# A gated recurrence over 256 tokens: doubling levels in place of sixteen sub-chunks and a chain of states

## Chip, cores and metric

One core of one Trainium2 chip runs the whole kernel. The metric is the device time of one execution in microseconds; the median of three runs is used. All data are fp32.

## The reference, cut to what matters

The model is two transformer blocks over 256 tokens of width 1024. The first has differential attention, a pooling mixer, 32 experts and an embedding gate. The second has windowed attention, a gated recurrence and 32 smaller experts. The change concerns the recurrence of the second block, four heads with 128 keys and 128 values:

```python
fg = lb + (1.0 - lb) * jax.nn.sigmoid(f_h)        # forget gates
hq = jax.nn.silu(q_h)
hk = 1.0 - fg
hlogf = jnp.log(fg)
hv = i_h
...
def step(state, inp):                             # chunks of 64 tokens
    b = jnp.cumsum(gc, axis=2)
    o_inter = jnp.einsum('bhtk,bhkv->bhtv', qc * jnp.exp(b), state)
    decay = jnp.exp(jnp.where(causal, b[t] - b[s], -jnp.inf))
    a = jnp.einsum('bhtk,bhsk,bhtsk->bhts', qc, kc, decay)
    o_intra = jnp.einsum('bhts,bhsv->bhtv', a, vc)
    state = jnp.exp(b_last) * state + (kc * jnp.exp(b_last - b))^T vc
...
ho = rms_norm_2(hgrn2_chunkwise(hq, hk, hv, hlogf), hgrn_norm_w)
hgrn = ho * jax.nn.silu(g_h)
mixed = sigmoid(z_a) * (attn @ w_branch_attn) + sigmoid(z_b) * (hgrn @ w_branch_hgrn)
x = x + mixed @ w_out
```

Written out, the output of token t is the sum over s up to t of (q_t · (product of the gates after s up to t) · k_s) v_s, the product being taken per key channel.

## The kernel before

The kernel is written by hand, engine by engine, with semaphores. Weights stream through a ring of six slots of 2 MB, filled by SyncE in a fixed order; each load waits until the last matmul that reads the slot's old content has run. The six slots serve first the projections of block one, then the experts of block one, then the seventeen loads of the middle, then the experts of block two. In block two an expert takes three slots, and each slot's next load waits for a count of TensorE's (`free[s]`). The first six expert loads wait for `dense2`, a count of finished dense products.

The middle of block two runs on TensorE as follows. Norm and transposes; twenty projections (`project(i)`, two row tiles for each piece of `w_in`), each eight matmuls of 128x512, into banks 0 to 3 in turn. ScalarE copies each out or takes its sigmoid (`leave(i)`). Between them stand the score matmuls of the attention, the transposes of its probabilities (L1583, copied by VectorE at L1056) and its products with the values (L1591).

The recurrence of before splits the 256 tokens into sixteen sub-chunks of 16 (`SUB`). Inside a sub-chunk it works by offset: for n = 0 to 15 VectorE forms the products of query and key of all token pairs whose key stands at one position (`offset(n)`, L1095 and L1099) and TensorE sums them over the keys' channels by a matmul with a shifted matrix of ones (`sums(n)`, L1615). Across sub-chunks a state of 128x128 for each head goes from one to the next: TensorE makes the update (`update(i)`, L1626), VectorE applies the gates (`state(i)`, L1114), and TensorE multiplies the state by the queries (`inter(i)`, L1635). The eight-plus-eight matmuls of the last piece of `w_in` (`last_projections`, L1649) are put one by one between these. Then the products of the pair matrix with the values (L1673) are added, the output is copied and transposed back (L1681), normalized on VectorE, and multiplied by the gate.

After it come the branch products from L1492, which is the line of the helper `dense` for every dense product of the middle, the transposes, the output projection, the router and the experts (gate and up at L1346, down at L1373).

Of the kernel before, what the change touches and what calls it, by code (L numbers as in the profile page):

```python
# [45 lines left out]
SUB = 16  # L46
NSUB = T // SUB
# [7 lines left out]
def two_blocks(nc, w, out):  # L55
# [11 lines left out]
    with ctx:  # L67
# [15 lines left out]
        blk = sb("blk", [P, P])  # L83
        spread = sb("spread", [P, P + SUB - 1])
# [3 lines left out]
        par = sb("par", [P, 2])  # L88
# [171 lines left out]
        k1, pre_f, suf_f, r_q, w_a, w_b, q_e, ke_even, ke_odd = (scr[:, 1024 * k:1024 * (k + 1)] for k in range(9))  # L260
        by_sub = "p (b j) -> p b j"
        states = xs[:, :, :].rearrange("p a n -> p (a n)").rearrange("p (k n) -> p k n", k=4)
# [60 lines left out]
        def _(pool):  # L323
# [20 lines left out]
            pool.memset(tri[:, :], 1.0)  # L344
            step(pool.memset(blk[:, :], 1.0))
# [4 lines left out]
            select(blk[:, :], ALU.is_ge, 0.0, 0, [[-SUB, P // SUB], [0, SUB]], 1)  # L350
            select(blk[:, :], ALU.is_ge, 0.0, SUB - 1, [[SUB, P // SUB], [0, SUB]], -1)
# [26 lines left out]
            step(pool.memset(spread[:, :], 0.0))  # L378
            pool.memset(spread[:, SUB - 1::SUB], 1.0)
# [12 lines left out]

            step(pool.tensor_copy(par[:, 1:2], blk[:, SUB:SUB + 1]))
            for k in (3, 5, 7):
                step(pool.tensor_tensor(par[:, 1:2], par[:, 1:2], blk[:, SUB * k:SUB * k + 1], ALU.add))
            pool.tensor_tensor(par[:, 0:1], ones[:, 0:1], par[:, 1:2], ALU.subtract).then_inc(sem("parity"), 1)
# [7 lines left out]
        def _(act):  # L404
# [205 lines left out]
            for a in range(TT):  # L610
                act.activation(xs[:, 1, 512 * a:512 * (a + 1)], Z[:, a, 1280:1792], ACT.Sigmoid).then_inc(sem("g_sig"), 1)

            act.wait_ge(sem("row_max"), 3)
            for g in range(8):
                act.activation(sA0[:, g, :], sA0[:, g, :], ACT.Exp, bias=qss[:, g:g + 1],
                               accum_out=qms[:, g:g + 1]).then_inc(sem("probs"), 1)
            for i in range(12, 16):
                leave(i)
            act.wait_ge(sem("row_max"), 4)
            for g in range(8):  # L620
                act.activation(sA1[:, g, :], sA1[:, g, :], ACT.Exp, bias=qss[:, 8 + g:9 + g],
                               accum_out=qms[:, 8 + g:9 + g]).then_inc(sem("probs"), 1)
            act.activation(qrt[:, 0:16], qrt[:, 0:16], ACT.Exp).then_inc(sem("sink_exp"), 1)
            for i in range(16, 20):
                leave(i)

            act.wait_ge(sem("hgrn_o"), 1)
            act.copy(w_b[:, 0:512], bank(0)).then_inc(sem("oT_act"), 1)
# [11 lines left out]
        def _(dve):  # L640
# [387 lines left out]
            step(tt(hq, hq, xs[:, 0, :], ALU.mult))  # L1028

# [13 lines left out]
            for a, sc in enumerate((sA0, sA1)):  # L1043
                m = qrs[:, 8 * a:8 * a + 8]
                step(dve.tensor_reduce(m, sc, X, ALU.max))
                step(tt(m, m, sinks[:, :], ALU.max))
                step(tt(qrt[:, 8 * a:8 * a + 8], sinks[:, :], m, ALU.subtract))
                ts(qss[:, 8 * a:8 * a + 8], m, -1.0, None, ALU.mult).then_inc(sem("row_max"), 1)
            dve.wait_ge(sem("g_sig"), 2)
            for a in range(TT):  # L1050
                v = Z[:, a, 1280:1792]
                step(tt(v, v, xs[:, 1, 512 * a:512 * (a + 1)], ALU.mult))

            for k in range(6):
                dve.wait_ge(sem("w_turned"), 3 + k + 1)
                dve.tensor_copy(pT2[:, 4 * k:4 * k + 4, :], bank(4 + k % 4).rearrange("p (g q) -> p g q", g=4))\  # L1056
                    .then_inc(sem("p2_copied"), 1)

            step(ts(k1, fg, -1.0, 1.0, ALU.mult, ALU.add))
            f_b, k_b, r_b = (v.rearrange(by_sub, j=SUB) for v in (fg, k1, r_q))  # L1060
            pf_b, sf_b = (v.rearrange(by_sub, j=SUB) for v in (pre_f, suf_f))
            wa_b, wb_b = (v.rearrange(by_sub, j=SUB) for v in (w_a, w_b))
            factor, start = xs[:, 0, :], xs[:, 1, :]
            factor_b, start_b = (v.rearrange(by_sub, j=SUB) for v in (factor, start))
            dve.tensor_copy(factor, fg)
            step(dve.memset(start, 0.0))
            dve.memset(factor_b[:, :, 0:1], 0.0)
            step(dve.tensor_copy(start_b[:, :, 0:1], f_b[:, :, 0:1]))
            step(dve.tensor_tensor_scan(pre_f, factor, start, 0.0, ALU.mult, ALU.add))
            step(dve.memset(sf_b[:, :, SUB - 1:SUB], 1.0))  # L1070
            for j in range(SUB - 1, 0, -1):
                step(tt(sf_b[:, :, j - 1:j], sf_b[:, :, j:j + 1], f_b[:, :, j:j + 1], ALU.mult))
            tt(suf_f, suf_f, k1, ALU.mult).then_inc(sem("ke_ready"), 1)
# [4 lines left out]
            for a in range(TT):  # L1078
                dve.wait_ge(sem("pv"), 2 + a + 1)
                tt(ao[:, a, :].rearrange("p (g d) -> p g d", d=64), bank(6 + a).rearrange("p (g d) -> p g d", d=64),  # L1080
                   qrs[:, 8 * a:8 * a + 8, None].broadcast_to([P, 8, 64]), ALU.mult).then_inc(sem("branch_ready"), 1)
            for a in range(TT):
# [3 lines left out]
            step(tt(q_e, hq, pre_f, ALU.mult))  # L1086

            step(dve.tensor_copy(r_q, hq))
            nb = TT * P * 4 // SUB

            def offset(n):
                j = SUB - 1 - n
                if n:
                    v = r_b[:, :, j + 1:SUB]
                    step(tt(v, v, f_b[:, :, j + 1:j + 2].broadcast_to([P, nb, SUB - 1 - j]), ALU.mult))  # L1095
                if n >= 2:
                    dve.wait_ge(sem("w_used"), n - 1)
                buf = (wa_b, wb_b)[n % 2]
                tt(buf[:, :, j:SUB], r_b[:, :, j:SUB], k_b[:, :, j:j + 1].broadcast_to([P, nb, SUB - j]), ALU.mult)\  # L1099
                    .then_inc(sem("w_offset"), 1)  # L1100

            def state(i):

                dve.wait_ge(sem("update"), i + 1)
                if i >= 4:
                    dve.wait_ge(sem("inter"), i - 3)
                new, old = states[:, (i + 1) % 4, :], states[:, i % 4, :]
                if i == 0:
                    dve.tensor_copy(new, bank(5)).then_inc(sem("state"), 4)
                    return  # L1110
                dve.wait_ge(sem("state"), 4 * i)
                for n in range(4):
                    r = slice(n * P, (n + 1) * P)
                    stt(out=new[:, r], in0=old[:, r], scalar=pre_f[:, n * T + SUB * i + SUB - 1:n * T + SUB * i + SUB],  # L1114
                        in1=bank(5 + 2 * (i % 2))[:, r], op0=ALU.mult, op1=ALU.add).then_inc(sem("state"), 1)

            offset(0)
            offset(1)
            dve.wait_ge(sem("parity"), 1)
            for a in range(TT):  # L1120
                dve.wait_ge(sem("ke_turned"), a + 1)
                for v, k in ((ke_even, 0), (ke_odd, 1)):
                    ts(v[:, 512 * a:512 * (a + 1)], bank(7 if a == 0 else 5), par[:, k:k + 1], None, ALU.mult)\
                        .then_inc(sem("ke_copied"), 1)
            for n in range(2, SUB):
                offset(n)
                state(n - 2)

            dve.wait_ge(sem("w_used"), SUB)
            for g in range(2):  # L1130
                tt(r_q[:, 512 * g:512 * (g + 1)].rearrange("p (g t) -> p g t", g=4), bank(4 + 2 * g).rearrange("p (g t) -> p g t", g=4),
                   blk[:, None, :].broadcast_to([P, 4, P]), ALU.mult).then_inc(sem("intra"), 1)
            state(NSUB - 2)
            dve.wait_ge(sem("hgrn_o"), 2)
            dve.tensor_copy(w_b[:, 512:1024], bank(1)).then_inc(sem("oT_dve"), 1)

            for a in range(TT):
                dve.wait_ge(sem("o_turned"), a + 1)
                step(dve.tensor_copy(k1[:, 512 * a:512 * (a + 1)], bank(6 + a)))
            o = k1.rearrange("p (g d) -> p g d", d=P)  # L1140
# [598 lines left out]
```

## Time and profile before

| | |
|---|---|
| median of 3 runs | 1975.18 us (1974.69 to 1977.14) |
| profiled execution | 1973.43 us |
| its span | 1971.7 us |
| TensorE matmul busy | 1776.4 us (90%) |
| VectorE busy | 429.3 us (22%) |
| ScalarE busy | 261.3 us (13%) |
| DMA, mean over the span | 339 GB/s |
| mean granted TensorE clock | 0.976 |

The profile cuts the span into 40 slices of 49.3 us; slices are counted from 0 here. Busy shares are averages over stages of very different kinds, so the chain of waits and the timelines of single stretches count for more. fp32 matmuls and their weight loads appear as two records each; transposes as one. The busy time of a matmul record overlaps its neighbours', so starts are compared, not durations added.

### The profile page before, as it was taken

To read this page: it belongs to the slowest core of one execution; us is meant where nothing else is said; L and a number is where in the kernel's file an instruction comes from. 1 tells how busy PE (TensorE), PEld (TensorE's weight loads), DVE (VectorE), ACT (ScalarE), POOL (GpSimd) and SP (SyncE) were. 2 spreads that over 40 slices of the span, in tenths; PEclk is the share of its full clock that TensorE was granted. 3 is DMA by queue.
4 is the path that set the end of the run, shared out by engine and by line. 5 is a ranking of instruction groups with operands and counts; after the bars stand their busy time and mean duration, and the time that the engine had idled before them with its cause. 6 is when DMAs were issued, how large, how long until landed. Compare 5 with 4: busy or idle time off the path is not lost.

```text
span 1971.7 us, 28706 instructions
## 1 busy us (share of the span) xinstructions
PE 1776.4 (90%) x12236; PEld 822.3 (42%) x12236; DVE 429.3 (22%) x1033; ACT 261.3 (13%) x534; POOL 24.4 (1%) x100
## 2 busy tenths in 40 slices
PE   7778999999999999999999988989988888888887
PEld 3444333333333333333333335647645555555554
DVE  1623111111111111111111123226523111111111
ACT  1210111111111111111111021130011111111111
POOL 3010000000000000000000000000000000000000
PEclk9888999999999999999999998999998999999999
DMA  9424999999999999999999783330144999999997
GB/s 302 177 75 176 429 428 429 428 428 429 427 430 427 429 428 428 429 428 428 428 429 429 308 298 128 128 128 1 69 150 157 428 429 427 429 428 429 428 428 309
DMA packets 69697, 667.73 MB, mean 339 GB/s; under 512 B 9392, under 2 KB 11200, under 8 KB 31648
## 3 DMA queue, kind: packets, MB, share of 16 engines
q1 hardware_dynamic: 64864, 664.84, 81.0%
q10 hardware_dynamic: 4416, 1.49, 0.3%
q0 software_dynamic: 384, 0.93, 0.2%
q8 instruction: 24, 0.39, 0.1%
q14 instruction: 9, 0.07, 0.0%
HBM read 666.19 MB, written 1.05 MB: 338 GB/s over the span
## 4 chain that ended last, share of the span: by engine, by line
DMA 50%; PE 43%; DVE 3%; ACT 1%; issue 1%; SPq 1%; DVEq 0%; ACTq 0%
DMA ring<-in_w_up 34%; DMA ring<-in_w_up_experts 16%; PE ps L1319 13%; PE ps L1492 11%; PE ps L1346 4%; PE ps L1198 3%; PE ps L1304 2%; PE ps L1373 2%; PE ps L1267 2%; PE ps L1615 1%; PE ps L1182 1%; PE ps L1626 1%; PE ps L1649 1%; PE ps L1392 1%; PE ps L1635 1%
## 5 line engine op out<-in xcount | busy, mean ns | idle before, releaser
L1319 PE MATMUL ps<-ring,Z 128*64 128x512 f32 x3168 | 710.3, 599 | 36.5 <-DMA ring<-in_w_up 35.8
L1319 PEld LDWEIGHTS ps<-ring,Z 128*64 128x64 f32 x3168 | 218.9, 137 | 501.6 <-issue 416.0
L1346 PE MATMUL ps<-ring,Z 128*32 128x128 f32 x4096 | 246.9, 408 | 64.4 <-DMA ring<-in_w_gate_experts 33.0
L1346 PEld LDWEIGHTS ps<-ring,Z 128*32 128x32 f32 x4096 | 148.4, 126 | 153.9 <-DMA ring<-in_w_up_experts 44.4
L1492 PE MATMUL ps<-ring,xT 128*128 128x512 f32 (+1 forms) x352 | 147.7, 580 | 1.5 <-DVE xT L662 0.8
L875 DVE TENSOR_SCALAR Z<-ps 128x512 f32<-128x512 f32 x33 | 22.8, 692 | 437.7 <-PE ps L1319 437.7
L1304 PE MATMUL ps<-xs,Z 128*32 128x256 f32 (+1 forms) x800 | 105.6, 476 | 4.5 <-DVE Z L847 4.5
L1492 PEld LDWEIGHTS ps<-ring,xT 128*128 128x128 f32 x352 | 67.5, 193 | 79.1 <-issue 76.2
L877 DVE TENSOR_SCALAR Z<-ps 128x512 f32<-128x512 f32 x33 | 22.8, 692 | 250.8 <-PE ps L1319 250.8
L887 DVE TENSOR_TENSOR Z<-Z,ps 128x128 f32<-128x128 f32 x32 | 9.2, 288 | 296.6 <-ACT Z L502 296.6
L515 ACT COPY Z<-ps 128x512 f32<-128x512 f32 (+1 forms) x65 | 31.2, 480 | 290.6 <-PE ps L1319 247.1
L506 ACT COPY Z<-ps 128x256 f32<-128x256 f32 x65 | 24.2, 372 | 340.5 <-PE ps L1354 340.5
L1392 PE MATMUL ps<-Z 64*128 64x512 f32 x264 | 65.6, 615 | 1.5 <-ACT Z L515 1.5
L1373 PE MATMUL ps<-ring,Z 128*32 128x256 f32 x1024 | 61.6, 379 | 0.0
L1198 PE MATMUL ps<-ring,xT 128*128 128x512 f32 x128 | 57.5, 612 | 0.8 <-DVE xT L662 0.8
L860 DVE TENSOR_TENSOR Z<-ps,gcol 128x512 f32<-128x512 f32 (+1 forms) x67 | 37.5, 560 | 83.7 <-PE ps L1313 83.5
L1304 PEld LDWEIGHTS ps<-xs,Z 128*32 128x32 f32 (+1 forms) x800 | 37.1, 126 | 41.7 <-issue 27.0
L1182 PE MATMUL ps<-ident,xs 128*128 128x128 f32 x112 | 21.0, 361 | 36.8 <-DVE xs L658 29.5
L499 ACT ACTIVATE Z<-Z 128x512 f32<-128x512 f32 x33 | 20.8, 630 | 238.4 <-DVE Z L875 238.4
L502 ACT ACTIVATE Z<-ps 128x128 f32<-128x128 f32 x32 | 8.9, 277 | 301.5 <-PE ps L1346 301.5
L868 DVE TENSOR_SCALAR Z<-iota,Z 128x128 f32<-128x128 f32 x130 | 38.9, 341 | 31.4 <-PE ps L1354 31.4
L1373 PEld LDWEIGHTS ps<-ring,Z 128*32 128x32 f32 x1024 | 36.9, 109 | 19.1 <-issue 0.2
(356 smaller groups left out, 1250.8 us busy)
## 6 DMA issues: line engine op xcount, KB each, us to landing
ring<-in_w_gate SPq DMA_DIRECT2D x66, 2048.0 KB, 23.0
ring<-in_w_up SPq DMA_DIRECT2D x66, 2048.0 KB, 25.6
ring<-in_w_down SPq DMA_DIRECT2D x66, 2048.0 KB, 21.4
ring<-in_w_gate_experts SPq DMA_DIRECT2D x32, 2048.0 KB, 17.0
ring<-in_w_up_experts SPq DMA_DIRECT2D x32, 2048.0 KB, 21.5
ring<-in_w_down_experts SPq DMA_DIRECT2D x32, 2048.0 KB, 13.0
ring<-in_w_in SPq DMA_DIRECT2D x13, 2048.0 KB, 9.6
ring<-in_w_out SPq DMA_DIRECT2D x4, 2048.0 KB, 17.3
```

The source lines that it names most:

```text
L515: act.copy(y[:, 0:(512, 256)[k]], bank((7, 5)[k])[:, 0:(512, 256)[k]]).then_inc(done_by(q, "act", "y"), 1)
L860: tt(picked[:, 0:DC * CAPS[k]].rearrange("p (c j s) -> p c j s", **by_chunk), bank(6)[:, 0:DC * CAPS[k]].rearrange("p (c j s) -> p c j s", ...
L868: ts(gated[:, a].rearrange("p (j s) -> p j s", s=CAPS[k]), iota[:, None, 0:CAPS[k]].broadcast_to([P, P // CAPS[k], CAPS[k]]), rank[:, a, d ...
L1182: last = pe.transpose(dst[:, i * P:(i + 1) * P], src[:, c + i:c + i + stride * (P - 1) + 1:stride], ident[:, :])
L1198: last = pe.matmul(bank((4 + j) % 8), xT[:, c, a * P:(a + 1) * P], slot(u, DC, 512)[:, c, :], start=c == 0, stop=c == DC - 1)
L1267: last = pe.matmul(bank((5, 6, 7, 0)[b]), xT[:, c, a * P:(a + 1) * P], slot(4 + n, DC, 512)[:, c, :], start=c == 0, stop=c == DC - 1)
L1304: last = pe.matmul(bank(6)[n * j:n * (j + 1), 0:P * c].rearrange("p (q c) -> p q c", c=c), one_hot[:, a, 0:n], xs[:, a, :].rearrange("p (q ...
L1319: last = pe.matmul(dst[CAP * j:CAP * (j + 1)], lhsT, rhs(j), start=start, stop=True, skip_group_check=True)
L1346: last = pe.matmul(bank(4)[CAP2 * t:CAP2 * (t + 1), P * s:P * (s + 1)], picked[:, chunk * CAP2:(chunk + 1) * CAP2], v[:, c, t:512:4], star ...
L1373: last = pe.matmul(bank(5)[CAP2 * t:CAP2 * (t + 1), 0:T], hid[:, CAP2 * j:CAP2 * (j + 1)], v[:, j, T * t:T * (t + 1)], start=j == 0, stop= ...
L1392: last = pe.matmul(bank(2 * a + j), back[CAP * j:CAP * (j + 1), a * P:(a + 1) * P], y[CAP * j:CAP * (j + 1), :], start=False, stop=True, s ...
L1492: last = pe.matmul(dst, lhs(c), rhs(c), start=c == 0, stop=c == nc_ - 1)
```

## The change

The recurrence is computed for all 256 tokens by doubling. `q_e` starts as query times own gate and `k_e` as one minus the gate. At level k the tokens are seen in pairs of blocks of 2^k. The product of `k_e` with the second blocks' `q_e` (one matmul of 128 by 128 by 64 for each head and row tile) holds the wanted entries for the pairs of that level; a mask `pair` of that level picks them into `own_A` by a predicated copy. Then `q_e` of the second blocks is multiplied by the gates' product over the first block, and `k_e` of the first blocks by that over the second; `totals` holds these products, halved in number at each level. Seven levels cover a row tile of 128. One set of products between the tiles (`cross_products`) and the diagonal (`own_products`, picked by multiplication with the identity) complete the matrix. Twelve matmuls with the values give the output in token rows, in banks 6 and 7, so it isn't transposed back.

Around it: projections use banks 0 and 1 in turn in place of 0 to 3; levels stand between the last projections on TensorE, the transposes of the probabilities are split in two and four; all exponentials of the attention stand ahead of projection 12's copy on ScalarE; the sum of squares of the output is ScalarE's; the norm's gain is multiplied into the gate beforehand; GpSimd builds `pair` in place of the block mask, the matrix of shifted ones and the parities.

```diff
+        q_e, k_e = xs[:, 0, :], xs[:, 1, :]
...
+            step(pool.memset(pair[:, :, :], 1.0))
+            for level in range(LEVELS - 1):
+                n = 2 ** level
+                v = pair[:, level, :].rearrange("p (b j) -> p b j", j=n)
+                select(v, ALU.is_ge, 0.0, 0, [[-2 * n, P // 2 // n], [0, n]], 1)
+                select(v, ALU.is_ge, 0.0, n - 1, [[2 * n, P // 2 // n], [0, n]], -1)
...
-                b, a = bank(i % 4), i % 2
+                b, a = bank(i % 2), i % 2
...
-            for i in range(12, 16):
+            for a, sc in enumerate((sA0, sA1)):
+                act.wait_ge(sem("row_max"), 3 + a)
+                for g in range(8):
+                    act.activation(sc[:, g, :], sc[:, g, :], ACT.Exp, bias=qss[:, 8 * a + g:8 * a + g + 1],
+                                   accum_out=qms[:, 8 * a + g:8 * a + g + 1]).then_inc(sem("probs"), 1)
+            act.activation(qrt[:, 0:16], qrt[:, 0:16], ACT.Exp).then_inc(sem("sink_exp"), 1)
+            for i in range(12, 18):
                 leave(i)
...
+            ts(k_e, fg, -1.0, 1.0, ALU.mult, ALU.add).then_inc(sem("level"), 1)
+            tt(q_e, hq, fg, ALU.mult).then_inc(sem("level"), 1)
...
+            def level(k):
+                size = 2 ** k
+                dve.wait_ge(sem("products"), k + 3)
+                dve.wait_ge(sem("level"), 2 * k + 2)
+                whole = totals[k].rearrange("p (b two) -> p b two", two=2)
+                n = whole.shape[1]
+                if k < LEVELS - 1:
+                    dve.tensor_tensor(totals[k + 1], whole[:, :, 0], whole[:, :, 1], ALU.mult).then_inc(sem("total"), 1)
+                for v, other in ((q_e, 0), (k_e, 1)):
+                    v = split(v, size)[:, :, 1 - other, :]
+                    tt(v, v, whole[:, :, other, None].broadcast_to([P, n, size]), ALU.mult).then_inc(sem("level"), 1)
+                if k < LEVELS - 1:
+                    dve.copy_predicated(split(own_A, size)[:, :, 1, :].rearrange("p (g b) j -> p g b j", g=8),
+                                        pair[:, k, None, :].bitcast(I32).broadcast_to([P, 8, P // 2]).rearrange("p g (b j) -> p g b j", j=size),
+                                        bank(2 + k % 2).rearrange("p (g b j) -> p g b j", g=8, j=size)).then_inc(sem("chosen_A"), 1)
+                else:
+                    dve.tensor_copy(split(own_A, size)[0:size, :, 1, :],
+                                    bank(2 + k % 2)[0:size, :].rearrange("p (g j) -> p g j", j=size)).then_inc(sem("chosen_A"), 1)
...
+            for a in range(TT):
+                v = Z[:, a, 1280:1792]
+                step(tt(v, v, g_sig[a], ALU.mult))
+                v = v.rearrange("p (g d) -> p g d", d=P)
+                tt(v, v, hnorm[:, None, :].broadcast_to([P, 4, P]), ALU.mult).then_inc(sem("g_silu"), 1)
+            for k in range(3):
+                level(k)
+            copy_p(range(2))
+            for k in range(3, 5):
+                level(k)
+            copy_p(range(2, 6))
+            level(5)
...
+            def products(k):
+                size = 2 ** k
+                pe.wait_ge(sem("level"), 2 * k + 2)
+                pe.wait_ge(sem("chosen_A"), k + 1)
+                rows = P if k < LEVELS - 1 else size
+                for n in range(4):
+                    for a in range(TT):
+                        g = n * TT + a
+                        last = pe.matmul(bank(2 + k % 2)[0:rows, g * 64:(g + 1) * 64].rearrange("p (b j) -> p b j", j=size),
+                                         tokens(k_e, n, a)[:, 0:rows], split(tokens(q_e, n, a), size)[:, :, 1, :],
+                                         start=True, stop=True)
+                last.then_inc(sem("products"), 1)
...
+            own_products()
+            project(11)
+            products(0)
+            project(12)
+            products(1)
+            project(13)
+            products(2)
+            turn_p(range(2))
+            project(14)
+            products(3)
+            project(15)
+            products(4)
+            turn_p(range(2, 6))
+            project(16)
+            products(5)
```

After these stand the products of probabilities and values, project(17), products(6), the transposes of the attention output, project(18), cross_products, project(19) and the products with the values; `offset`, `state`, `sums`, `update`, `inter` and `last_projections` are gone.

## Rows read from the trace of the kernel before

**Rows 1.** The page: DMA share by slices, and the chain by engine.
```profile
DMA  9424999999999999999999783330144999999997
...
DMA 50%; PE 43%; DVE 3%; ACT 1%; issue 1%; SPq 1%; DVEq 0%; ACTq 0%
```

**Rows 2.** The chain that ended last, in order: start us, us, what.
```profile
1268.94 41.41 PE ps L1492 x96
...
1333.87 5.32 PE ps L1591 x48
...
1351.89 0.61 PE ps L1615 x4
...
1353.39 0.80 PE ps L1635 x8
...
1406.43 1.88 PE ps L1673 x16
...
1411.05 13.75 PE ps L1492 x32
...
1549.36 21.79 DMA ring<-in_w_up_experts
```

**Rows 3.** SyncE's queue: first, last preload of experts, and the seventh load.
```profile
1405.66 0.33 SPq L283 DMA_DIRECT2D ring<-in_w_gate_experts  x1
...
1472.31 0.43 SPq L283 DMA_DIRECT2D ring<-in_w_down_experts  x1
1506.24 0.34 SPq L288 DMA_DIRECT2D ring<-in_w_gate_experts  x1
```

**Rows 4.** Busy us by stretch: length, PE, PEld, DVE, ACT, POOL, clock, DMA.
```profile
1343.60:1411.00 67.40, 66.47 (x365) 49.99 (x366) 41.62 (x95) 3.06 (x4) 0.00 (x0) 0.97 0.07 24
1411.00:1502.00 91.00, 75.33 (x245) 38.26 (x243) 37.43 (x104) 8.02 (x17) 1.80 (x2) 0.92 0.33 123
```

**Rows 5.** Groups by line, TensorE, 1343 to 1411 us.
```profile
L1615 PE MATMUL ps<-scr,spread 128*128 128x32 f32 (+15 forms) x64 | 20.0, 436 | 1.0 <-DVE scr L1099 1.0
...
L1626 PE MATMUL ps<-Z,scr 32*128 32x128 f32 x120 | 17.0, 282 | 0.0
```

**Rows 6.** TensorE's timeline: start, us, group, and the idle before it.
```profile
1310.17 1.04 PE L1583 MATMUL ps<-ident,scr 128*128 128x128 f32 x8
1316.38 3.68 PE L1583 MATMUL ps<-ident,scr 128*128 128x128 f32 x16 [5.17 <-ACT scr L621]
...
1341.58 1.06 PE L1604 MATMUL ps<-ident,scr 128*128 128x128 f32 x8 [0.88 <-DVE Z L1084]
1343.65 0.79 PE L1615 MATMUL ps<-scr,spread 128*128 128x32 f32 x4 [1.01 <-DVE scr L1099]
```

**Rows 7.** Line L1591: duration ns, minimum, median, maximum.
```profile
L1591 PEld LDWEIGHTS ps<-Z,scr x48: 190/192/192, 1333.3 to 1338.8; 128*128 128x128 f32 x48
```

**Rows 8.** VectorE's timeline.
```profile
1266.46 1.29 DVE L1032 SCALAR_TENSOR_TENSOR scr<-ps,mask_win 128x512 f32<-128x512 f32 x2 [10.80 <-PE ps L1557]
...
1284.70 1.42 DVE L1052 TENSOR_TENSOR Z<-Z,xs 128x512 f32<-128x512 f32 x2 [9.79 <-ACT xs L611]
...
1317.53 0.69 DVE L1056 COPY scr<-ps 128x512 f32<-128x512 f32 x1 [5.36 <-PE ps L1583]
```

**Rows 9.** ScalarE's timeline.
```profile
1283.52 1.15 ACT L611 ACTIVATE xs<-Z 128x512 f32<-128x512 f32 x2
1284.69 1.28 ACT L615 ACT_TABLE_LOAD   x1
...
1312.79 0.49 ACT L621 ACTIVATE scr<-scr,st 128x256 f32<-128x256 f32 x1
```

**Rows 10.** As rows 4, short stretches: the granted clock is third from the end.
```profile
1318.00:1320.00 2.00, 2.00 (x11) 2.00 (x10) 1.60 (x3) 0.00 (x0) 0.00 (x0) 0.50 0.48 181
...
1345.00:1347.00 2.00, 2.00 (x7) 1.24 (x6) 1.97 (x5) 0.00 (x0) 0.00 (x0) 0.50 0.00 0
...
1380.00:1390.00 10.00, 10.00 (x55) 7.49 (x55) 6.72 (x15) 0.00 (x0) 0.00 (x0) 1.00 0.00 0
```

More of the change, by code:

```diff
@@ L259, in two_blocks, with split @@
         hq, fg = Z[:, 0, 3840:4864], Z[:, 1, 3840:4864]
-        k1, pre_f, suf_f, r_q, w_a, w_b, q_e, ke_even, ke_odd = (scr[:, 1024 * k:1024 * (k + 1)] for k in range(9))
-        by_sub = "p (b j) -> p b j"
-        states = xs[:, :, :].rearrange("p a n -> p (a n)").rearrange("p (k n) -> p k n", k=4)
+        q_e, k_e = xs[:, 0, :], xs[:, 1, :]
+        own_A = scr[:, 0:1024]
+        cross_A = scr[:, 7424:7936].rearrange("p (n t) -> p n t", n=4)
+        o2 = scr[:, 2304:3328]
+        o2_sq = scr[:, 3328:4352]
+        g_sig = [Z[:, a, 3328:3840] for a in range(TT)]
+        def split(v, size):
+            return v.rearrange("p (b two j) -> p b two j", two=2, j=size)
+        totals, at = [fg], 0
+        for level in range(LEVELS - 1):
+            n = T * 4 >> (level + 1)
+            totals.append(hq[:, at:at + n])
+            at += n
         full = [sem(f"slot_full{s}") for s in range(SLOTS)]
@@ L1102, in state @@
[L1102 to L1115, printed above, removed]
@@ L1130, in _ @@
[L1130 to L1139, printed above, removed]
@@ L1585, in _, with tokens, own_products @@
-            for i in range(16, 18):
-                project(i)
+            project(10)
+            def tokens(v, n, a):
+                return v[:, n * T + a * P:n * T + (a + 1) * P]
+            def own_products():
+                pe.wait_ge(sem("level"), 1)
+                for a in range(TT):
+                    for n in range(4):
+                        last = pe.matmul(bank(2 + a)[:, n * P:(n + 1) * P], tokens(k_e, n, a), tokens(hq, n, a), start=True, stop=True)
+                    last.then_inc(sem("products"), 1)
@@ new lines, in cross_products, with turn_p @@
+            def cross_products():
+                pe.wait_ge(sem("level"), 2 * LEVELS + 2)
+                pe.wait_ge(sem("chosen_A"), LEVELS + 1)
+                for n in range(4):
+                    last = pe.matmul(bank(3)[:, n * P:(n + 1) * P], tokens(k_e, n, 0), tokens(q_e, n, 1), start=True, stop=True)
+                last.then_inc(sem("products"), 1)
+            def turn_p(ks):
+                for k in ks:
+                    g0 = 4 * (k % 2)
+                    if k == 0:
+                        pe.wait_ge(sem("scores2_copied"), 6)
+                    if k in (0, 2):
+                        pe.wait_ge(sem("probs"), 24 if k == 0 else 32)
+                    if k >= 4:
+                        pe.wait_ge(sem("p2_copied"), k - 3)
+                    for i in range(4):
+                        src = sA0[:, g0 + i, :] if k < 2 else sA1[:, g0 + i, (k // 2 - 1) * P:(k // 2) * P]
+                        last = pe.transpose(bank(4 + k % 4)[:, i * P:(i + 1) * P], src, ident[:, :])
+                    last.then_inc(sem("w_turned"), 1)
@@ L1608, in sums @@
-            def sums(n):
-                j = SUB - 1 - n
-                pe.wait_ge(sem("w_offset"), n + 1)
-                buf = (w_a, w_b)[n % 2].rearrange(by_sub, j=SUB)
-                nb = 512 // SUB
-                for g in range(2):
-                    last = pe.matmul(bank(4 + 2 * g).rearrange(by_sub, j=SUB)[:, :, j:SUB], spread[:, n:n + P],
-                                     buf[:, nb * g:nb * (g + 1), j:SUB], start=n == 0, stop=True, skip_group_check=True)
-                last.then_inc(sem("w_used"), 1)
@@ L1619, in update @@
-            def update(i):
-                if i >= 2:
-                    pe.wait_ge(sem("state"), 4 * (i - 1))
-                a, r = i // 8, slice(32 * (i // 2 % 4), 32 * (i // 2 % 4) + 32)
-                src = (ke_even, ke_odd)[i % 2]
-                for n in range(4):
-                    last = pe.matmul(bank(5 + 2 * (i % 2))[:, n * P:(n + 1) * P], src[r, 512 * a + n * P:512 * a + (n + 1) * P],
-                                     Z[r, a, 768 + n * P:768 + (n + 1) * P], start=True, stop=True)
-                last.then_inc(sem("update"), 1)
@@ L1630, in inter @@
-            def inter(i):
-                pe.wait_ge(sem("state"), 4 * i)
-                for n in range(4):
-                    lo = (n % 2) * T + SUB * i
-                    last = pe.matmul(bank(n // 2)[:, lo:lo + SUB], states[:, i % 4, n * P:(n + 1) * P],
-                                     q_e[:, n * T + SUB * i:n * T + SUB * (i + 1)], start=False, stop=True,
-                                     skip_group_check=True)
-                    if i == NSUB - 1 and n % 2 == 1:
-                        last.then_inc(sem("hgrn_o"), 1)
-                if i < NSUB - 1:
-                    last.then_inc(sem("inter"), 1)
@@ L1643, in last_projections @@
-            def last_projections(n):
-                a, c = n // DC, n % DC
-                if c == 0:
-                    pe.wait_ge(*middle_full(12))
-                    pe.wait_ge(sem("d2_copied"), 15 + a)
-                last = pe.matmul(bank(2 + a), tile(a)(c), slot(12 % SLOTS, DC, 512)[:, c, :], start=c == 0, stop=c == DC - 1)
-                if c == DC - 1:
-                    last.then_inc(sem("dense2"), 1)
-            sums(0)
-            last_projections(0)
-            sums(1)
@@ L1656, in _ @@
-            last_projections(1)
-            pe.wait_ge(sem("ke_copied"), 4)
-            pe.wait_ge(sem("d2_copied"), 18)
-            for b in range(2):
-                pe.matmul(bank(b), zeros[:, :], q_e[:, 0:512], start=True, stop=True)
-            update(0)
-            update(1)
-            for n in range(2, SUB):
-                sums(n)
-                last_projections(n)
-                inter(n - 1)
-                if n < NSUB - 1:
-                    update(n)
-            pe.wait_ge(sem("intra"), 2)
@@ L1684, in _ @@
+                    last = pe.matmul(out_o, by_tile[:, n, a, :], Z[:, a, v_n], start=True, stop=a == 0)
+                    if a == 1:
+                        last = pe.matmul(out_o, cross_A[:, n, :], Z[:, 0, v_n], start=False, stop=True)
+                last.then_inc(sem("hgrn_o"), 1)
             pe.wait_ge(*middle_full(13))
             pe.wait_ge(sem("d2_copied"), 20)
+            pe.wait_ge(sem("branch_copied"), 2)
             v_a, v_h = slot(13 % SLOTS, 4, 1024), slot(14 % SLOTS, 4, 1024)
```

168 lines of the change are left out of this document (53 added, 115 removed).

## Prediction

> **What bounds the kernel now.** I read the page first. Half of the chain that ended last is DMA and most of the rest is TensorE [rows 1]. The slices of the DMA line say where: the two stages of experts run with the DMA engines full, and between them, in slices 24 to 30, the engines are mostly idle. The change lies in that middle. So the first question is whether time won there reaches the end, for some 430 us of transfers stand behind it.
>
> The chain in order of time answers it [rows 2]. From 1268.9 us to 1411.1 us it is TensorE almost alone. Later, inside the second expert stage, it becomes transfers of in_w_up_experts, 21.8 us a piece. The queue of SyncE shows what starts these transfers [rows 3]. The first six fill the ring while the middle still runs (issued at 1405.7 to 1472.3 us). The seventh is issued at 1506.2 us, when TensorE has freed slot 0 with the first expert's gate matmuls. All later ones hang on it. Nothing in the stream starts at a time of its own: each wait counts something TensorE has done. If the branch products start earlier by x, the six preloads, the first expert and the seventh transfer all come earlier by x, and so does the end. Between the sixth preload and the seventh transfer lie 34 us, and the DMA engines are busy for a third of the time around them [rows 4], so the ring is full when the first expert starts, and stays so when all of it moves together.
>
> Then the stretch itself. Between the end of the score matmuls (1268.9) and the first branch product (1411.1) lie 142.1 us. TensorE is busy for 66.5 of the last 67.4 us, VectorE for 41.6 [rows 4]: the recurrence is not bound by VectorE, it is made of TensorE's small matmuls. In it stand, one by one, the 16 matmuls of the last two projections (L1649). They remain.
>
> **The change, part by part.** I compute TensorE's work between the same two points afterwards, then check that no other engine is late.
>
> One fp32 matmul is two records. Kept work: ten projections. Six of them are 41.4 us [rows 2], 6.9 us each, so 69.0 us. The transposes of the probabilities are 24; eight take 1.04 us where nothing waits [rows 6], so 3.1 us. The probability-value products are 5.3 us (5.5 with the tail), the eight transposes of the attention output 1.0 us. Sum kept: 78.4 us.
>
> Added work. The level products have 128 stationary and 64 moving columns. The nearest row has just that shape: L1591, 24 matmuls in 5.3 us, 0.222 us each [rows 2]. Seven levels by eight matmuls: 56 x 0.222 = 12.4 us. (The seventh has 64 stationary columns; I give it no discount.) The own-token products (8), the cross products (4) and the products with the values (12) are 128x128. L1673 has eight of those in 1.88 us, 0.235 us each [rows 2], so 24 x 0.235 = 5.6 us. Added: 18.0 us. All together 96.4 us in place of 142.1.
>
> Removed, as a cross-check: the sums (20.0 us by records), updates (17.0), the states into outputs, the zeroing, the old value products and two rounds of transposes, by records that overlap a little [rows 5]; in chain time it is 67.4 us less 13.8 for two projections, 53.6 us. Before it, 1.0 us of transposes of the decayed keys and 1.9 us of waits; and 5.2 us of waiting for eight exponentials at 1311 us, with 1.6 us more because the 16 transposes behind it took 3.7 us [rows 6]. That is 63.3 us, less 18.0 added: 45.3. The two ways agree within 0.5 us.
>
> Bounds of the small matmul. Low: with 16 moving columns eight records take 0.80 us, 0.20 us a matmul [rows 2], so the levels are 1.2 us cheaper. High: the two 96-column sums between other kinds of matmul took 0.61 us, 0.305 each [rows 2], 4.7 us dearer. I take L1591's value because it has the same shape and also runs in a group.
>
> TensorE: Matmul & The Clock Gate of the Trainium skill (LDWEIGHTS) says that a weight load lasts by the columns of the stationary operand, about P/1.2 ns. With two passes that is 0.213 us a matmul and an estimate of 11.9 us for the levels. By the moving columns alone it would be half. The trace agrees with the load: L1591's took 192 ns a record [rows 7], and overlap.
>
> **Does VectorE keep up?** By the order in the diff, own products stand at 1275.8, projection 11 ends at 1284.6, products(0) at 1286.4, projection 12 at 1293.2, products(1) at 1295. The rest follow at about 1303, 1313, 1322, 1332 and 1346 us, and the cross products at 1354.
>
> A level on VectorE is two multiplications of 512 elements (0.69 us each), one of at most 512 for the totals, and a predicated copy out of PSUM [rows 8]. No row shows a predicated copy. Below: a copy of 512 from PSUM, 0.69 us. Above: 1.4 us, if the destination has to be read in a second pass (twice that row). I take 0.7; a level is then 2.1 to 2.8 us. It has a projection of 6.9 us to hide under. The tightest place is level 0. It stands behind the gate multiplications, which wait for the sigmoids of g: ScalarE ends them at 1286.4 (two of 0.58 behind projection 11's copy), the four multiplications by gate and norm take 2.8 us, and three more of 0.69 finish k_e and q_e at 1291.3. TensorE asks at 1293.2: 1.9 us spare. The next tightest is level 4 with four copies of probabilities, 1.4 + 0.2 + 0.7 + 4 x 0.69 = 5.1 us in a gap of 10.7 us. A predicated copy would have to exceed 6 us to delay anything there. The two operations of 1024 elements added ahead of the scores (at most 2.8 us, four times a row of 512) lie in 10.8 us of idle time [rows 8].
>
> **ScalarE.** With two banks in place of four, a projection waits for the copy of the one before the last. That copy takes 0.6 us and has 6.9 us. One spot is different: all sixteen exponentials now stand ahead of copy 12. From 1286.4: a table load 1.3, sixteen of at most 0.49, one small one, a table load 1.3 and the copy 0.6 [rows 9] give 1298 at the latest. Projection 14, which needs it, starts at 1304.5. Spare 6.5 us or more. So the wait of 5.2 us at 1311 goes and none takes its place.
>
> **After the recurrence.** Output leaves as token rows, so two copies and eight transposes go. The square is ScalarE's, the reduction, root and three multiplications come to about 6 us, against 13.9 us of branch products on TensorE. It was hidden before and is hidden still. From the first branch product on the intervals stay. SyncE issues the same loads against the same counts. GpSimd builds twelve small masks in the first block, right behind its router loads, as it built the parities; nobody needs them before 1289 us. The instructions that it loses at the start I cost at nothing: VectorE's early work there ends in a wait for the small loads.
>
> **Clock.** The granted clock was 0.50 from 1316 to 1320 us, behind the idle 5.2 us, and 0.50 again from 1345 to 1347, behind short waits [rows 10]; elsewhere in the stretch 1.00, the 2.4 GHz level. My durations are from the full level. Since I find no wait left on TensorE, I keep them.
>
> **Sum.** 142.1 - 96.4 = 45.7 us. The profiled execution took 1973.4 us (span 1971.7), so 1927.7. The median of the runs is 1.8 us above it: 1929.5 us. Below 0.2% (4 us) a measurement of this kernel can't tell from no change.
>
> **The rivals.**
> A, 78%: TensorE is the bound and the small matmuls cost as in the rows: 1924 to 1937, likeliest 1929.5. The upper end takes the 0.305 us matmul and 3 us of small waits at the fourteen new hand-overs.
> B, 13%: VectorE's levels show. For: every level is a round trip (products, multiplications, next products), and level 0 has only 1.9 us. Against: each later round has a projection over it. If half of each level (1.2 us) were seen seven times, with some half-clock time behind each, some 15 us come back: 1938 to 1950.
> C, 3%: the gain is hidden by the transfers behind it. It would need the seventh expert transfer to be late for a reason of its own, such as queueing behind the preload. Against: 34 us between them, and a DMA share of 0.07 from 1343.6 to 1411 us [rows 4]. Then 1971 to 1977.
> D, 4%: slower. The clock. For: the two short waits at 1341 to 1344 us (0.9 and 1.0 us) were enough for a granted clock of 0.50 behind them [rows 6, 10], and the new order has a semaphore at every hand-over. At the half level each us of TensorE's work costs one more. The 96.4 us would become up to 193, which is 1973.4 + 50.7, or 2026 us against the median. It decides from 46 us of full-speed work run at half clock. Against: in the old recurrence there were three semaphores every 4 us for 60 us and the clock stayed at 1.00 [rows 10].
> The Trainium skill names this rival too (TensorE: Matmul & The Clock Gate, A second HAM failure mode: psum-queue depth-cycling): frequent micro-idles between matmul groups make the clock swing. Its rule and the dips of [rows 10] agree; that the new hand-overs leave such idles is not shown by any row.
> E, 2%: a far faster one, the level products at the price of their moving columns (half of 0.222): 1923.
>
> The range runs from 1922 to 1940, A and E with the lower part of B. Faster 0.94, same 0.02, slower 0.04.
>
> **What would show it.** After the change, TensorE between the scores and the first branch product: 96 us, idle under 2 us, clock 1.00. Groups of eight level products of 1.8 us, seven times; predicated copies near 0.7 us; VectorE idle before each waiting for TensorE, not the other way round. TensorE waiting for VectorE at products(1) would mean B; a clock of 0.5 in the 1290 to 1360 us window D; an expert transfer that is no longer 95 us behind the first branch product C. I am wrong if a level product costs over 0.3 us or a predicated copy over 6.

## The result

The kernel after takes 1930.3 us (median of 4 runs, 1929.9 to 1930.8) against 1976.1 us before on the same occasion. The ratio is 0.9777, 95% interval 0.9764 to 0.9789: the difference of the two medians is 45.8 us. (The ratio is formed from the single runs and is not the quotient of the medians, which is 0.9768.) The forecast was 1929.5. Its profiled execution took 1930.75 us, with a span of 1929.0. One of the eight executions of before beside the last four kernels below took 5143.6 us, in a slow state; it counts in their median of 1974.5 us (1973.7 without it) but not in the ratios.

TensorE's timeline of the kernel after, from the last score matmuls to the first branch product, answers to [rows 2, 6]. Columns: start us, us, engine, line, operation, shapes, count, and idle before it in brackets.

```profile
1272.10 7.13 PE L1479 MATMUL ps<-ring,xT 128*128 128x512 f32 x16
1279.07 1.95 PE L1567 MATMUL ps<-Z,xs 128*128 128x128 f32 x16
1280.86 7.03 PE L1479 MATMUL ps<-ring,xT 128*128 128x512 f32 x16
1287.72 1.90 PE L1579 MATMUL ps<-xs 128*128 128x64 f32 x16
1289.46 7.08 PE L1479 MATMUL ps<-ring,xT 128*128 128x512 f32 x16
1296.38 1.90 PE L1579 MATMUL ps<-xs 128*128 128x64 f32 x16
...
1324.90 1.92 PE L1603 MATMUL ps<-ident,scr 128*128 128x128 f32 x16
1326.65 7.03 PE L1479 MATMUL ps<-ring,xT 128*128 128x512 f32 x16
1333.52 1.89 PE L1579 MATMUL ps<-xs 128*128 128x64 f32 x16
1335.25 5.52 PE L1625 MATMUL ps<-Z,scr 128*128 128x64 f32 x48
1340.61 7.08 PE L1479 MATMUL ps<-ring,xT 128*128 128x512 f32 x16
1347.63 1.15 PE L1579 MATMUL ps<-xs 128*64 128x64 f32 x16
...
1367.08 13.90 PE L1479 MATMUL ps<-ring,Z 128*128 128x512 f32 x32
```

There isn't one bracket between 1272.10 and 1367.08: TensorE never waits. The stretch lasts 94.98 us. The same view of before has these two ends, 142.02 us apart:

```profile
1268.87 41.47 PE L1492 MATMUL ps<-ring,xT 128*128 128x512 f32 x96
...
1410.89 13.90 PE L1492 MATMUL ps<-ring,Z 128*128 128x512 f32 x32
```

So the change takes 47.0 us out of its own stretch. The branch products start 43.8 us earlier, the whole span is 42.7 us shorter. The difference of some 4 us lies outside the change; I come to it with the last experiment.

VectorE's timeline of the kernel after, levels 0 to 2 and the four copies of probabilities behind level 4, answers to [rows 8]. An instruction's end is its start plus its time.

```profile
1292.39 0.69 DVE L1072 TENSOR_TENSOR Z<-Z 128x512 f32<-128x512 f32 x1
1292.99 1.29 DVE L1075 TENSOR_TENSOR xs<-xs,Z 128x512 f32<-128x512 f32 x2
1294.20 1.30 DVE L1077 COPY_PREDICATED scr<-pair,ps 128x512 f32<-128x512 int32 x1
1298.48 0.43 DVE L1072 TENSOR_TENSOR Z<-Z 128x256 f32<-128x256 f32 x1 [2.98 <-PE ps L1579]
1298.82 1.29 DVE L1075 TENSOR_TENSOR xs<-xs,Z 128x512 f32<-128x512 f32 x2
1300.02 1.29 DVE L1077 COPY_PREDICATED scr<-pair,ps 128x512 f32<-128x512 int32 x1
1307.13 0.29 DVE L1072 TENSOR_TENSOR Z<-Z 128x128 f32<-128x128 f32 x1 [5.82 <-PE ps L1579]
1307.34 1.28 DVE L1075 TENSOR_TENSOR xs<-xs,Z 128x512 f32<-128x512 f32 x2
1308.55 0.69 DVE L1077 COPY_PREDICATED scr<-pair,ps 128x512 f32<-128x512 int32 x1
...
1327.32 2.48 DVE L1061 COPY scr<-ps 128x512 f32<-128x512 f32 x4
```

(The prediction counted from before's 1268.9 us; this trace reaches the stretch 3.2 us later.) It is VectorE that waits for TensorE: 3.0 us before level 1, 5.8 before level 2. Level 0's `k_e` is done at 1294.3, TensorE asks at 1296.4: 2.1 us spare where I had counted 1.9.

Busy time and clock by stretch, kernel after, answers to [rows 4].

```profile
1272.10:1367.10 95.00, 95.00 (x403) 56.39 (x402) 33.35 (x57) 17.49 (x48) 0.00 (x0) 1.00 0.26 85
1431.00:1460.00 29.00, 20.24 (x92) 14.16 (x92) 15.87 (x72) 3.61 (x9) 0.00 (x0) 0.59 0.30 130
```

TensorE is busy for 95.0 of 95.0 us at a granted clock of 1.00. SyncE's queue answers to [rows 3]: the seventh expert transfer is issued 97.3 us behind the first branch product (before: 95.3). The prediction had named a distance other than 95 us as a sign of rival C. The 2 us lie in the router's stretch, where the granted clock was 0.59 and the first group of the router's matmuls took 7.04 us against 5.32 before; in the second trace of the same kernel (after_again) the distance is 95.6 us. So it isn't the sign that was meant.

```profile
1428.51 0.43 SPq L293 DMA_DIRECT2D ring<-in_w_down_experts  x1
1464.35 0.34 SPq L298 DMA_DIRECT2D ring<-in_w_gate_experts  x1
```

### The profile page after: what moved, and what is told of

It is laid out like the page before. It is cut to its first block, busy times and chain, and to the rows that moved or that the text cites. A ratio compares the mean times of both kernels' runs of the same rounds, so it can differ in the third digit from the quotient of the medians.

```text
span 1929.0 us, 28248 instructions
## 1 busy us (share of the span) xinstructions
PE 1744.8 (90%) x12056; PEld 798.3 (41%) x12056; DVE 392.6 (20%) x943; ACT 259.3 (13%) x533; POOL 27.3 (1%) x104
## 4 chain that ended last, share of the span: by engine, by line
DMA 51%; PE 43%; DVE 3%; ACT 1%; issue 1%; SPq 1%; DVEq 0%; ACTq 0%
DMA ring<-in_w_up 34%; DMA ring<-in_w_up_experts 17%; PE ps L1306 13%; PE ps L1479 12%; PE ps L1333 4%; PE ps L1185 3%; PE ps L1291 2%; PE ps L1360 2%; PE ps L1254 2%; PE ps L1169 1%; PE ps L1379 1%; PE ps L1264 1%; SPq L298 1%; PE ps L1579 1%; PE ps L1316 0%
## 5 line engine op out<-in xcount | busy, mean ns | idle before, releaser
L1479 PE MATMUL ps<-ring,xT 128*128 128x512 f32 (+1 forms) x384 | 163.0, 582 | 1.5 <-DVE xT L669 0.8
L1479 PEld LDWEIGHTS ps<-ring,xT 128*128 128x128 f32 x384 | 72.8, 192 | 83.0 <-issue 80.2
L875 DVE TENSOR_SCALAR Z<-iota,Z 128x128 f32<-128x128 f32 x130 | 38.9, 341 | 31.4 <-PE ps L1341 31.4
```

The costliest lines, as they stand in the source:

```text
L875: ts(gated[:, a].rearrange("p (j s) -> p j s", s=CAPS[k]), iota[:, None, 0:CAPS[k]].broadcast_to([P, P // CAPS[k], CAPS[k]]), rank[:, a, d ...
L1479: last = pe.matmul(dst, lhs(c), rhs(c), start=c == 0, stop=c == nc_ - 1)
```

## The experiments

Two theories stand behind most of them. T: TensorE bounds the stretch, and the change is worth the work and the waits that it takes from TensorE. B: VectorE's levels are at the edge. In the table, "stretch" is the time from the first projection behind the scores to the first branch product, read from each kernel's TensorE timeline, and "idle" the sum of TensorE's waits in it. In the last column the ratio to before has its 95% interval.

| kernel | stretch us | idle us | median us | ratio to before |
|---|---|---|---|---|
| before | 142.02 | 8.2 | 1976.1 | |
| after | 94.98 | 0 | 1930.3 | 0.9777 (0.9764 to 0.9789) |
| exps_alone (on before) | 134.85 | 3.0 | 1966.5 | 0.9955 (0.9938 to 0.9971) |
| projections_first | 110.60 | 7.2 | 1945.4 | 0.9853 (0.9836 to 0.9869) |
| products_twice | 106.64 | 0 | 1939.4 | 0.9825 (0.9809 to 0.9841) |
| exps_late | 101.63 | 4.3 | 1934.9 | 0.9793 (0.9777 to 0.9809) |
| copies_4 | 94.98 | 0 | 1924.7 | 0.9751 (0.9735 to 0.9768) |
| copies_10 | 119.63 | 12.8 | 1951.0 | 0.9885 (0.9868 to 0.9901) |
| turn_before_last | 94.98 | 0 | 1927.1 | 0.9763 (0.9744 to 0.9781) |
| after_again | 94.98 | 0 | 1925.0 | 0.9763 (0.9745 to 0.9782) |

Before was 1975.3 us beside exps_alone, projections_first, products_twice and exps_late, and 1974.5 us beside the last four. Only the last three had the kernel after run beside them, so the others are compared with it by their stretches, not by medians.

**The exponentials alone**, on the kernel before.

```diff
+            act.wait_ge(sem("row_max"), 4)
+            for g in range(8):
+                act.activation(sA1[:, g, :], sA1[:, g, :], ACT.Exp, ...)
+            act.activation(qrt[:, 0:16], qrt[:, 0:16], ACT.Exp).then_inc(sem("sink_exp"), 1)
             for i in range(12, 16):
                 leave(i)
-            act.wait_ge(sem("row_max"), 4)
...
```

> The kernel before with one part of the change alone: all sixteen exponentials of the attention stand ahead of projection 12's copy on ScalarE. Theory T (TensorE bounds the stretch, and the change is worth the TensorE work and waits it takes away, term by term): the wait of 5.2 us before the last 16 transposes goes and they take 2.1 us again instead of 3.7, so 6.8 us faster, 0.4% (5 to 8 us). Rival R (the waits were slack that the old recurrence would have absorbed, the gain is all in the recurrence): within 2 us of before.

The stretch is 7.2 us shorter. The whole is 0.45% faster; the interval is some 6 to 12 us, so rival R is out. The profiled execution was the slowest of the four: its span is 1971.8 us, as long as before's 1971.7. Its stretch begins 2.9 us later than before's, and its router stretch, at a lower granted clock, takes more time; such differences come back in the last experiment. TensorE's timeline of this kernel shows the 24 transposes in one go where [rows 6] has a wait of 5.17 us:

```profile
1313.04 2.78 PE L1583 MATMUL ps<-ident,scr 128*128 128x128 f32 x24
```

T holds; a seventh of the change's gain is this edit.

**The opposite: exponentials late**, on the kernel after. ScalarE makes copies 12 to 15 before the second eight exponentials.

```diff
             for a, sc in enumerate((sA0, sA1)):
+                if a == 1:
+                    for i in range(12, 16):
+                        leave(i)
                 act.wait_ge(sem("row_max"), 3 + a)
...
-            for i in range(12, 18):
+            for i in range(16, 18):
                 leave(i)
```

> The kernel after with one part undone: the second eight exponentials stand again behind the copies 12 to 15 on ScalarE. Theory T: projection 15 ends at 1323.2 us; copy 0.6, table load 1.3, eight exponentials 3.9 give 1329.2; TensorE wants the transposes at 1324.9, so a wait of 4.3 us and a halved clock behind it: 4.3 to 8 us slower than after. Rival R (slack elsewhere absorbs it): within 2 us of after.

The stretch is 6.7 us longer. TensorE's timeline and two short stretches of this kernel:

```profile
1329.27 3.68 PE L1606 MATMUL ps<-ident,scr 128*128 128x128 f32 x16 [4.31 <-ACT scr L627]
```

```profile
1329.00:1331.00 2.00, 1.73 (x8) 1.74 (x9) 0.48 (x1) 1.60 (x4) 0.00 (x0) 0.50 1.02 387
1331.00:1333.00 2.00, 2.00 (x11) 2.00 (x10) 1.61 (x4) 0.00 (x0) 0.00 (x0) 0.50 0.43 168
```

The wait is 4.31 us as computed. Nearly all of the other 2.3 us goes with the lower granted clock behind it (0.50, the 1.2 GHz level, while the 16 transposes run): they take 3.68 us where they took 1.92, and the projection behind them takes 7.50 us where it took 7.03. This wait cost about half as much again.

**Every level's matmuls twice.** The output is unchanged, the work on TensorE grows.

```diff
-                for n in range(4):
+                for n in range(8):
+                    n %= 4
                     for a in range(TT):
```

> The kernel after with each level's matmuls issued twice, to the same place: 56 more. Theory T: TensorE sets the time of the stretch, so each costs its full 0.216 us (0.134 for the eight with 64 stationary columns): 48 x 0.216 + 8 x 0.134 = 11.4 us slower than after (10.5 to 12.5). Rival B (VectorE's levels set the time): less than 6 us, since the extra matmuls of a level delay VectorE but overlap its chain.

The stretch grows by 11.66 us, and TensorE still has no wait in it. Each added matmul costs its full price; B, which had less than 6 us, falls.

**Projections first.** The same instructions, but nothing between the levels.

```diff
             own_products()
-            project(11)
+            for i in range(11, 20):
+                project(i)
             products(0)
-            project(12)
             products(1)
-            project(13)
             products(2)
             turn_p(range(2))
-            project(14)
...
```

> The kernel after with the same instructions in another order on TensorE: own products, then projections 11 to 19 in one go, then the levels one after the other with nothing between them but the attention's transposes and value products. Theory T: the work is the same, but the projections no longer cover the round trip of a level. TensorE waits per level for the totals, two multiplications and the semaphores: about 2.2 us at level 0 and 1.6 at the later ones, some 12 us, more where the copies of probabilities stand in between (4 us), and as much again by a halved granted clock on the small matmuls behind these waits (up to 12 us): 15 to 28 us slower than after, so still 18 to 30 us faster than before. Rival R (the interleaving is what won the time): 40 us or more slower than after, at before's time. Rival S (levels overlap anyway): within 4 us of after.

The stretch is 15.6 us longer than after's, at the low end of T. TensorE's timeline, and one short stretch, of this kernel:

```profile
1338.94 1.89 PE L1579 MATMUL ps<-xs 128*128 128x64 f32 x16
1342.99 3.37 PE L1579 MATMUL ps<-xs 128*128 128x64 f32 x16 [2.15 <-DVE xs L1075]
...
1348.25 3.68 PE L1579 MATMUL ps<-xs 128*128 128x64 f32 x16 [1.89 <-DVE xs L1075]
1351.72 1.91 PE L1603 MATMUL ps<-ident,scr 128*128 128x128 f32 x8
```

```profile
1348.00:1351.00 3.00, 2.75 (x13) 2.75 (x14) 1.39 (x2) 0.00 (x0) 0.00 (x0) 0.50 0.00 0
```

Now the brackets name VectorE (L1075, the multiplications, and for the last wait L1120, the copy of the cross products): TensorE waits 2.15, 1.89 and 1.52 us before three of the levels, and 0.2 and 1.4 us before the cross products and the value products, 7.2 us in all. Of the other 8.4 us, 7.6 are level products and transposes that ran at the lower clock: eight level products take 3.68 us where they took 1.90. This is rivals B and D of the prediction at work, in an order that the change doesn't have. It also splits the gain: 31.4 us of the 47.0 come without any projection to cover the levels (the exponentials' 7.2 among them), 15.6 us from standing between the projections.

**The predicated copy, 4 and 10 times.** It writes the same data each time.

```diff
-                    dve.copy_predicated(...).then_inc(sem("chosen_A"), 1)
+                    for again in range(4):
+                        ins = dve.copy_predicated(...)
+                        if again < 3:
+                            step(ins)
+                    ins.then_inc(sem("chosen_A"), 1)
```

> The kernel after with each predicated copy made four times (same data each time), 18 more on VectorE: 6 at 1.3 us and 12 at 0.7 us, 16 us of work. Theory T: every level has idle time of 3 to 7 us before it on VectorE, and the copy stands behind the multiplications that TensorE waits for, so nothing reaches TensorE: within 2 us of after. Rival B (VectorE is at the edge): 8 to 16 us slower.

> The kernel after with each predicated copy made ten times: 18 more at 1.3 us and 36 more at 0.7 us, 49 us of work on VectorE. Theory T puts the threshold near 6 us a level: levels 0 and 1 now take 15 us each against 8.7 us of TensorE work between their calls, levels 2 to 5 9 us each, two of them with copies of probabilities besides. VectorE's chain from 1292 us becomes about 70 us where it has 45: 18 to 32 us slower than after, with part of it by a halved clock. Rival S (VectorE has still more slack): under 8 us. Rival B: the full 49 us.

With four the stretch is 94.98 us, to the hundredth that of after. With ten it is 24.7 us longer, within the forecast's 18 to 32; VectorE's and TensorE's timelines of copies_10:

```profile
1293.06 13.28 DVE L1078 COPY_PREDICATED scr<-pair,ps 128x512 f32<-128x512 int32 x10
1306.37 0.42 DVE L1072 TENSOR_TENSOR Z<-Z 128x256 f32<-128x256 f32 x1
```

```profile
1308.05 3.06 PE L1583 MATMUL ps<-xs 128*128 128x64 f32 x16 [4.00 <-DVE xs L1075]
...
1322.78 2.00 PE L1583 MATMUL ps<-xs 128*128 128x64 f32 x16 [1.66 <-DVE xs L1075]
...
1332.71 2.00 PE L1583 MATMUL ps<-xs 128*128 128x64 f32 x16 [1.00 <-DVE xs L1075]
...
1351.19 10.51 PE L1629 MATMUL ps<-Z,scr 128*128 128x64 f32 x48 [6.13 <-DVE scr L1061]
```

Four waits, 12.8 us, and 11.9 us more, nearly all of it in groups at the lower clock behind them (the value products take 10.5 us in place of 5.5). So the levels hide copies of 2.9 to 5.3 us (four times 0.7 or 1.3), and do not hide copies of 7.3 to 13.3 us. The 6 us that the prediction gave for level 4 lie between, and no run places the threshold closer. An estimate from the trace of after agrees with them: behind level 4 the copies of probabilities end at 1329.8 us and the value products ask for them at 1335.3, so a copy of 0.7 us could grow by 5.5 us, to 6.2.

**Transposes ahead of the last branch product**, a version meant to be faster.

```diff
             for b in range(4):
                 a, n = b // 2, b % 2
+                if b == 3:
+                    ... the eight transposes of o2
                 dense(bank(b), ...)
-            ... the eight transposes of o2
```

with the two copies on VectorE likewise ahead of the fourth multiplication.

> A version meant to beat after: the eight transposes of the recurrence's output stand ahead of the fourth branch product on TensorE, and their copies ahead of its multiplication on VectorE. In after TensorE waits 1.12 us for these copies at 1382 us. Theory T: the output is ready at 1372.5 us, the third branch product ends at 1377.4, so nothing waits and the 1.1 us go: 0.5 to 1.5 us faster than after, at the edge of what can be measured. Rival: within 0.3 us, because the time comes back as a later wait or a different dip of the clock.

In its place it does what it should: TensorE's timeline has no wait where after waits 1.12 us.

```profile
1376.58 1.12 PE L1659 MATMUL ps<-ident,scr 128*128 128x128 f32 x8
1377.54 17.33 PE L1480 MATMUL ps<-ring,Z 128*128 128x512 f32 x40
```

From the first branch product to the output projection it needs 31.93 us against 33.29 in after, 1.4 us less. The medians, measured side by side, are 1927.1 and 1925.0 us, and the interval of each ratio reaches some 3.7 us to either side: whether the kernel as a whole is faster stays open.

**The kernel after once more.**

> The kernel after once more, on this chip, so that the others have it beside them: 0.977 of before. Its trace also shows whether the two dips of the granted clock outside the changed stretch (at 1110 us and in the router behind the middle), which cost the profiled execution some 5 us against the one of before, belong to the kernel or to the execution. If to the execution, they move by a few us between traces.

Its span is 1920.6 us, 8.4 us less than in the first trace of the same program. The stretch is the same to the hundredth. The 8.4 us lie in four places: 4.3 us before the first projection, 2.2 us in the projections before the scores, 1.6 us in the router behind the middle, and 0.2 us in the experts. Near the end of the first expert stage, the kernel after, first trace, has these pieces in TensorE's timeline and by stretch:

```profile
1112.46 1.98 PE L1316 MATMUL ps<-Z 32*64 32x512 f32 x8 [0.86 <-DVE Z L867]
1114.37 16.11 PE L1306 MATMUL ps<-ring,Z 128*64 128x512 f32 x64
```

```profile
1110.00:1114.00 4.00, 2.67 (x12) 1.03 (x12) 1.20 (x3) 0.42 (x1) 0.00 (x0) 0.50 1.01 430
1114.00:1118.00 4.00, 4.00 (x14) 1.16 (x12) 0.00 (x0) 0.00 (x0) 0.00 (x0) 0.50 1.02 426
```

and its second trace:

```profile
1108.53 1.09 PE L1316 MATMUL ps<-Z 32*64 32x512 f32 x8 [0.86 <-DVE Z L867]
1109.55 13.95 PE L1306 MATMUL ps<-ring,Z 128*64 128x512 f32 x64
```

```profile
1110.00:1114.00 4.00, 4.00 (x22) 1.40 (x20) 0.00 (x0) 0.00 (x0) 0.00 (x0) 1.00 1.02 426
```

The same two groups of matmuls, behind the same wait of 0.86 us, took 18.0 us where the granted clock began at 0.50 and 15.0 us where it was 1.00. So these dips belong to the execution. That also makes up the difference between the 47.0 us of the stretch and the 42.7 us of the spans of the first pair of traces: there the trace of before began its projections at 1199.8 us, that of after at 1203.0, and the router cost after 1.9 us more; the experts gave back 0.7.

## Why the prediction was right

The forecast named TensorE's work between two points as the whole matter, and its terms came out as follows; the measured ones are the intervals of after's chain of waits, of which some lines:

```profile
1272.17 7.06 PE ps L1479 x16
1279.23 1.78 PE ps L1567 x16
...
1287.89 1.73 PE ps L1579 x16
...
1325.06 1.75 PE ps L1603 x16
...
1335.41 5.36 PE ps L1625 x48
...
1347.70 1.08 PE ps L1579 x16
1348.77 1.16 PE ps L1633 x8
```

| term | predicted us | measured us |
|---|---|---|
| ten projections | 69.0 | 69.1 |
| 56 level products | 12.4 | 11.5 |
| own, cross and value products (24) | 5.6 | 5.3 |
| 24 transposes of probabilities | 3.1 | 2.6 |
| products of probabilities and values | 5.3 | 5.4 |
| eight transposes | 1.0 | 1.2 |
| waits | 0 | 0 |
| sum | 96.4 | 95.1 |

(The chain's intervals end 0.1 us later than the starts in the timeline, which give 94.98.)

- **The bound.** Right: nothing on TensorE waits in the stretch, and products_twice shows that an added matmul costs its full time (11.66 us for 11.4 expected).
- **The small matmul.** 0.216 us against the 0.222 of L1591. The seventh level, to which I gave no discount, was sized wrong: 0.134 us each, 1.08 us in place of 1.8. Its stationary operand has 64 columns. The Trainium skill's rule (TensorE: Matmul & The Clock Gate, LDWEIGHTS), that a weight load lasts by the columns of the stationary operand, fits the direction: the weight-load records fell from 192 to 133 ns. By the rule's P/1.2 ns twice, an estimate, those eight would have taken 0.85 us; they took 1.08. The prediction called the 192 ns of L1591's load record an agreement. The record is longer than the rule's 107 ns; what comes near it is half the interval between two level products, 108 ns.
- **VectorE.** Right: the slack at level 0 is 2.1 us for 1.9, and the threshold is not contradicted. The predicated copy was bounded by 0.69 and 1.4 us and put at 0.7; it takes 1.30 us at levels 0 and 1, near the upper bound, and 0.70 at the others. It hides either way, as copies_4 shows.
- **ScalarE.** Right: the copy of projection 12 was done at 1300.1 us, projection 14 asked at 1307.6.
- **The transfers behind it.** Rival C falls: the first branch product comes 43.8 us earlier and the first expert's gate matmuls (1502.2 before, 1460.2 after) 42.0 us. From there to the end it is 468.8 us against 469.5.
- **The clock.** Rival D falls for this order, because there is no wait to set it off. Its mechanism is real: exps_late, projections_first and copies_10 pay 2.3, 8.4 and 11.9 us more behind waits of 4.3, 7.2 and 12.8 us in all, most of it in groups at a granted clock of 0.50.
- **Luck.** The stretch gave 1.3 us more than forecast, and the rest of the profiled execution 4.3 us less. The prediction took the rest to be unchanged, so its profiled time (1927.7) was missed by 3.0 us, and that the median was missed by only 0.8 us is luck: what the dips outside the change do to an execution is larger (8.4 us between two of one program). Against the 1925.0 us of after_again it would have missed by 4.5 us.

## What to carry to other kernels

Where one engine is busy throughout a stretch, price a change by that engine's work between two fixed points, with intervals between starts of the nearest shape, and use the other engines only to check that nobody is late. A chain of round trips between two engines is free if each trip has work of its own length to stand under; taking that cover away cost 15.6 us here, about half of it at the lower clock. In the three kernels that brought waits back, a wait on TensorE cost more than its length. Compare a stretch inside the traces before you believe a difference of a few us between whole executions.

## What was not expected of the hardware

- The time of one and the same program varied by 8.4 us of span between two executions on this evidence, all of it outside the changed stretch; where the traces were read closely, the same instructions ran at a granted clock of 0.50 in one and of 1.00 in the other, in a place where both had the same wait of 0.9 us. The Trainium skill (TensorE: Matmul & The Clock Gate, Part 1) says that the number of slow matmuls at a kernel's start varies from run to run of one kernel. The two traces show such a variation in the middle of a kernel; no run here shows it at the start.
- The predicated copy of 512 elements takes 1.30 us where the runs of its pattern are one or two elements long, and 0.70 us from four on. The multiplications on the same patterns took 0.69 us at every level. I have no experiment that says why.
- Repeated to the hundredth of a us, the stretch of 95 us had the same length in four traces (after, after_again, copies_4, turn_before_last): where TensorE neither waits nor dips, it is exact.
